# A result row for every choice of a token: plain scatters, six rows summed in the tail, three experts by one-hot products

## The reference, cut to what matters

```python
scores = sigmoid(xt @ router_w)                          # 512 x 64
_, sel = lax.top_k(scores + router_bias, 6)
wsel = scores[sel] / sum(scores[sel]) * 2.5
# each expert e, for the tokens that chose it:
gu = x[tok] @ w_gate_up[e]                               # 1024 -> 512
h = silu(gu[:, :256]) * gu[:, 256:]
y = (h @ w_down[e]) * w                                  # 256 -> 1024
routed[tok] += y
x = layer_norm(ALPHA * x + (routed + shared), ln2_g, ln2_b)
```

## Time and profile before

| | us |
|---|---|
| median of three runs | 1338.55 (1337.31 to 1342.82) |
| profiled execution, its own time | 1341.28 |
| its span on the core | 1339.6 |
| TensorE busy | 1238.4 (92%) |
| VectorE, ScalarE, GpSimd busy | 457.9, 311.3, 398.5 |
| 16 DMA engines, hardware queue of SP | 52.4% |
| 16 DMA engines, software queue of GpSimd | 7.8% |

### The profile page before, as it was taken

The page is one execution under the profiler, slowest core; times in us unless marked ns, Lnnn a source line. Parts: engine busy times, 40 slices in busy tenths (PEclk is TensorE's granted clock), DMA queues, the critical chain, the costliest instruction groups (busy, mean ns, idle before and its releaser), DMA issues.

```text
span 1339.6 us, 23794 instructions
## 1 busy us (share of the span) xinstructions
PE 1238.4 (92%) x8545; PEld 778.1 (58%) x8546; DVE 457.9 (34%) x923; ACT 311.3 (23%) x829; POOL 398.5 (30%) x424
## 2 busy tenths in 40 slices
PE   8999999999999989999999999987789979979896
PEld 5587778877774458888558654443344435534442
DVE  3755665556415443323248211111011111101115
ACT  3332333423313442222231111011111011101111
POOL 2545534355504340000000333233223322233321
PEclk9999999999999999999999899988899999989998
DMA  4621112115024223335904599999999998999995
GB/s 129 185 62 55 55 47 70 55 55 172 1 64 122 57 58 96 85 95 188 422 34 141 214 379 402 399 394 397 395 405 396 397 398 347 353 400 397 393 339 197
DMA packets 117965, 296.42 MB, mean 221 GB/s; under 512 B 11976, under 2 KB 81736, under 8 KB 101360
## 3 DMA queue, kind: packets, MB, share of 16 engines
q1 hardware_dynamic: 100384, 267.75, 52.4%
q0 software_dynamic: 15344, 25.12, 7.8%
q10 hardware_dynamic: 2144, 2.22, 0.5%
HBM read 280.93 MB, written 26.51 MB: 230 GB/s over the span
## 4 chain that ended last, share of the span: by engine, by line
PE 35%; DMA 21%; DVE 3%; issue 3%; POOL 1%; POOLq 0%; SPq 0%; ACT 0%; DVEq 0%; ACTq 0%
PE bank L1380 11%; PE bank L1980 10%; DMA sum_rows<-expert_y,row_col 8%; DMA expert_gu<-in_expert_w_gate_up_dram 6%; PE bank L1987 5%; PE bank L1386 4%; DMA sum_rows<-over_y,over_row_col 4%; DMA expert_down<-in_expert_w_down_dram 2%; PE bank L1972 1%; PE bank L2054 1%; PE bank L1408 1%; PE bank L2032 1%; PE bank L1401 1%; DMA gathered_x<-x_rows,tok_col 0%; DVE x_rows L2246 0%
## 5 line engine op out<-in xcount | busy, mean ns | idle before, releaser
L1980 PE MATMUL bank<-expert_gu,gathered_xT 128*64 128x256 f32 x2016 | 250.1, 400 | 31.7 <-DMA expert_gu<-in_expert_w_gate_up_dram 21.7
L1980 PEld LDWEIGHTS bank<-expert_gu,gathered_xT 128*64 128x64 f32 x2016 | 141.3, 138 | 121.8 <-issue 22.3
L2180 DVE SCALAR_TENSOR_TENSOR hidden<-gate,slot_w,bank 128x128 f32<-128x128 f32 x64 | 22.2, 347 | 434.1 <-ACT gate L2138 423.0
L1987 PE MATMUL bank<-expert_down,hiddenT 128*64 128x512 f32 x504 | 126.4, 623 | 18.7 <-issue 18.0
L1877 POOL DMA_INDIRECT sum_rows<-expert_y,row_col x62 | 98.2, 1584 | 47.9 <-POOL row_col L1874 46.3
L486 PE MATMUL bank<-x_high,w_head_low 128*128 128x512 f32 x224 | 93.8, 419 | 0.0
L486 PE MATMUL bank<-x_low,w_head_high 128*128 128x512 f32 x224 | 93.4, 417 | 0.0
L486 PE MATMUL bank<-x_high,w_head_high 128*128 128x512 f32 x224 | 93.4, 417 | 0.0
L1874 POOL COPY row_col<-row_idx 128x1 int32 (+1 forms) x62 | 12.0, 194 | 258.3 <-DMA sum_rows<-expert_y,row_col 136.9
L2149 ACT COPY expert_y<-bank 128x512 f32<-128x512 f32 x63 | 36.9, 585 | 180.2 <-PE bank L1987 104.3
L2138 ACT ACTIVATE gate<-bank 128x128 f32<-128x128 f32 x64 | 17.9, 279 | 247.9 <-PE bank L1980 247.9
(11 more groups left out here) (388 smaller groups left out, 2233.5 us busy)
## 6 DMA issues: line engine op xcount, KB each, us to landing
expert_gu<-in_expert_w_gate_up_dram SPq DMA_DIRECT2D x63, 2048.0 KB
expert_down<-in_expert_w_down_dram SPq DMA_DIRECT2D x63, 1024.0 KB
w_head<-in_w_in_dram SPq DMA_DIRECT2D x32, 512.0 KB, 3.9
w_tile<-in_w_in_dram SPq DMA_DIRECT2D x14, 512.0 KB, 4.2
x_rows<-in_x_dram SPq DMA_DIRECT2D x8, 512.0 KB, 6.5
sum_rows<-zero_rows SPq DMA_DIRECT2D x2, 2048.0 KB, 12.1
w_tile<-in_w_branch_a_dram SPq DMA_DIRECT2D x7, 512.0 KB, 5.7
w_pair<-in_w_in_dram SPq DMA_DIRECT2D x6, 512.0 KB, 5.5
```

What stands on the lines that cost most here:

```text
L1980: mm = nc.tensor.matmul(bank[parts[a], 0:2 * P], x[:, c, part], halves[:, a, :, :], start=(c == 0), stop=(c == KC - 1))
L1987: mm = nc.tensor.matmul(bank[parts[a], :], hidden_t[:, c * BLK:(c + 1) * BLK], dn[:, c, a * (D // 2):(a + 1) * (D // 2)], start=(c == 0), ...
```

## The change

- The two sum tensors become one, `choice_rows`, with 6 x 1024 half rows: every token has its own rows for each of its six choices. `tok` gets 512 k added for choice k, so `row_idx` points at the choice's own row; the token lists are masked back to the token with a bitwise and.
- The scatter is plain: no `compute_op`, and no wait for the scatter two steps before. The same holds for overflow blocks.
- Zeroing: six pieces of 2 MB, one in each round of the head loop.
- `DIRECT = 3`: experts 61, 62 and 63 go by one-hot products. Each result is split in a high part (ScalarE) and a rest (VectorE, `low_y`), and the products run in fp32r.
- Tail: SP loads for each tile four rows a token (`late`), then two (`first_rows`). GpSimd adds three of the six (`add_middle`), VectorE adds two to `xs` (`add_first`), and TensorE adds the remaining one and both sums into the banks (`finish_tile`). VectorE's order is add 0, add 1, normalise 0, add 2, normalise 1, add 3, normalise 2, normalise 3.

```diff
+TOKEN_BITS = int(OOB) | SEQ - 1
+TOKEN_HALF_BITS = 2 * int(OOB) | SUMS - 1
...
+            sp.wait_ge(zero_ready, 1)
             with sp.Fori(2, HEADS) as m:
...
-            sp.wait_ge(zero_ready, 1)
-            for a in sums:
-                n = a.shape[0] // P
-                sp.dma_start(a.rearrange("(n p) c -> p n c", p=P),
-                             zero[:, :].unsqueeze(1).broadcast_to([P, n, D // 2])).then_inc(zeroed, 16)
+                sp.dma_start(choice_rows[bass.ds(m * SUMS - 2 * SUMS, SUMS), :].rearrange("(n p) c -> p n c", p=P),
+                             zero[:, :].unsqueeze(1).broadcast_to([P, SUMS // P, D // 2])).then_inc(zeroed, 16)
...
-            sp.wait_ge(zeroed, 32)
+            sp.wait_ge(zeroed, 16 * TOPK)
...
-            mm = nc.vector.tensor_scalar(T["tok_idx"][part, :], ps[4][part, bass.ds(a, NE // 2, 2)], OOB, None, ALU.add)
-        mm.then_inc(idx_ready, 1)
+            then(nc.vector.tensor_scalar(T["tok_idx"][part, :], ps[4][part, bass.ds(a, NE // 2, 2)], OOB, None, ALU.add))
+        nc.vector.tensor_scalar(T["tok_idx"][:, :], T["tok_idx"][:, :], TOKEN_BITS, None, ALU.bitwise_and).then_inc(idx_ready, 1)
...
-    DIRECT = 2
+    DIRECT = 3
...
+    by_choice = choice_rows.rearrange("(k t p a) c -> t p k (a c)", k=TOPK, t=TT, p=P)
+    late = [at(f"late_rows{t}", [P, 4, D], r) for t, r in enumerate(("dnT", "bias", "dnl", "xh"))]
+    middle_rows, last_rows = [r[:, 0:3, :] for r in late], [r[:, 3:4, :] for r in late]
...
         for t in range(TT):
-            sp.dma_start(even_sums[:, t, :], token_rows[0][t, :, :]).then_inc(sums_in[0][t], 16)
-        for k in (1, 3):
-            sp.wait_ge(scattered[k], 16 * (NE // GROUP - k // 2))
-        for t in range(TT):
-            sp.dma_start(odd_sums[:, t, :], token_rows[1][t, :, :]).then_inc(sums_in[1][t], 16)
+            if t == 3:
+                sp.wait_ge(h_psum[1], NE // GROUP)
+            sp.dma_start(late[t][:, :, :], by_choice[t, :, 2:TOPK, :]).then_inc(late_in[t], 16)
+            if t == 2:
+                sp.wait_ge(y_psum[1], NE // GROUP)
+            if t == 3:
+                sp.wait_ge(h_psum[2], NE // GROUP)
+            sp.dma_start(first_rows[t][:, :, :], by_choice[t, :, 0:2, :]).then_inc(first_in[t], 16)
...
             pool.wait_ge(y_ready[k], now)
-            if not alone:
-                before, then_ = block_at(i, s - 2)
-                pool.wait_ge(scattered[before], 16 * then_)
...
-                out=sums[s % 2][:, :], out_offset=bass.IndirectOffsetOnAxis(ap=col2[:, k:k + 1], axis=0),
-                in_=y[:, k, :], in_offset=None, bounds_check=last_row, oob_is_err=False,
-                compute_op=ALU.add).then_inc(scattered[k], 16)
+                out=choice_rows[:, :], out_offset=bass.IndirectOffsetOnAxis(ap=col2[:, k:k + 1], axis=0),
+                in_=y[:, k, :], in_offset=None, bounds_check=last_row, oob_is_err=False).then_inc(scattered[k], 16)
...
+        def add_middle(t):
+            pool.wait_ge(late_in[t], 16)
+            for k in range(1, 3):
+                if k > 1:
+                    pool.wait_ge(middle_added, 2 * t + 1)
+                nc.gpsimd.tensor_tensor(middle_rows[t][:, 0, :], middle_rows[t][:, 0, :], middle_rows[t][:, k, :],
+                                        ALU.add).then_inc(middle_added, 1)
...
+        for t in range(TT - 1):
+            add_middle(t)
+        add_beta(0)
+        add_middle(TT - 1)
+        add_beta(1)
...
+        def direct(t, n, start=False):
+            pe.wait_ge(y_low, n + 1)
+            for part in (y_high[n], y_rest[n]):
+                for a in range(2):
+                    nc.tensor.matmul(z_banks[t][a][:, :], hot_row[parts[a], n, t * P:(t + 1) * P].bitcast(F32R),
+                                     part[parts[a], :].bitcast(F32R), start=(start and part is y_high[n]), stop=False)
...
+        def finish_tile(t):
+            pe.wait_ge(late_in[t], 16)
+            add_rows(t, last_rows[t][:, 0, :])
+            pe.wait_ge(middle_added, 2 * t + 2)
+            add_rows(t, middle_rows[t][:, 0, :])
+            pe.wait_ge(first_added, 2 * t + 2)
+            add_rows(t, xs[:, t, :], True).then_inc(z_psum, 1)
...
+        def low_y(s):
+            k, now = block_at(TURNS - 1, s)
+            n = s - (STEPS - DIRECT)
+            dve.wait_ge(y_ready[k], now)
+            nc.vector.tensor_tensor(y_rest[n][:, :].bitcast(F32R), ps[6 + k % 2][:, :], y_high[n][:, :],
+                                    ALU.subtract).then_inc(y_low, 1)
...
+        def add_first(t):
+            dve.wait_ge(first_in[t], 16)
+            for k in range(2):
+                if k:
+                    dve.wait_ge(first_added, 2 * t + 1)
+                nc.vector.tensor_tensor(xs[:, t, :], xs[:, t, :], first_rows[t][:, k, :], ALU.add).then_inc(first_added, 1)
```

More of the change, by code:

```diff
@@ L1898, in later @@
                     gather_later(j + 2, j + 2)
-                    if not alone:
-                        before, then_ = block_at(i, s - 3)
-                        pool.wait_ge(scattered[before], 16 * then_)
                     pool.wait_ge(over_y, j + 2)
@@ L1915, in turn @@
                     gather(i + 1, s // 2)
-                later(i, s, first and s < 3)
+                later(i, s)
                 if not (first and s == 0) and not (last and s > STEPS - DIRECT):
-                    scatter(i, s - 1, first and s < 3)
+                    scatter(i, s - 1)
         def first_gather(q):
@@ L2109, in tensor @@
+        pe.wait_ge(rows_ready, 5)
+        for n in (1, 0, 2):
             for t in range(TT - 1):
-                direct(t, n)
+                direct(t, n, n == 1)
+        finish_tile(0)
         pe.wait_ge(over_added, 1)
-        for n in range(DIRECT):
-            direct(TT - 1, n)
-        for t in range(TT - 1):
-            rows(t)
-        for t in range(TT - 1):
-            odd(t)
-        rows(TT - 1)
-        odd(TT - 1)
+        for n in (1, 0, 2):
+            direct(TT - 1, n, n == 1)
@@ L2121, in scalar @@
+        for t in range(1, TT):
+            finish_tile(t)
     def scalar(act):
@@ L2132, in later, with take_y, turn @@
                     nc.scalar.copy(yo[:, :], shared[:, :]).then_inc(over_y, 1)
-        def turn(i, first=False):
+        def take_y(b, direct):
+            out_y = y_high[b - (GROUP - DIRECT)][:, :].bitcast(F32R) if direct else y[:, b, :]
+            nc.scalar.copy(out_y, ps[6 + b % 2][:, :]).then_inc(y_ready[b], 1)
+        def turn(i, first=False, last=False):
             for s in range(STEPS):
@@ L2148, in turn @@
                         act.wait_ge(scattered[b], 16 * (then_ - 1))
-                    nc.scalar.copy(y[:, b, :], ps[6 + b % 2][:, :]).then_inc(y_ready[b], 1)
+                    take_y(b, last and s > STEPS - DIRECT)
                 act.wait_ge(h_psum[k], now)
@@ L2158, in scalar @@
         act.wait_ge(scattered[b], 16 * (then_ - 1))
[L2159 removed]
+        take_y(b, True)
         nc.scalar.preload_act_table_set(LN_EXP)
@@ L2213, in turn @@
                 later(i, s)
+                if last and s > STEPS - DIRECT:
+                    low_y(s - 1)
                 if shared_too and s < TT:
@@ L2328, in program @@
         x1_rows = nc.dram_tensor("x1_rows", [SEQ, D], F32, kind="Internal").ap()
-        sums = [nc.dram_tensor(f"sum_rows{n}", [SUMS, D // 2], F32, kind="Internal").ap() for n in range(2)]
+        choice_rows = nc.dram_tensor("choice_rows", [TOPK * SUMS, D // 2], F32, kind="Internal").ap()
         attention = ctx.enter_context(ExitStack())
```

103 lines of the change are left out of this document (52 added, 51 removed).

## The result

| | before | after |
|---|---|---|
| median, us | 1339.33 (1337.31 to 1342.82) | 1326.08 (1322.56 to 1327.03) |
| profiled execution, own time / span | 1341.28 / 1339.6 | 1322.56 / 1320.9 |
| last down weights used at (span time) | 1304.06 | 1269.73 |
| from there to the end | 35.5 | 51.2 |
| software queue, 740 to 1300 us before, 740 to 1260 us after | 17.7% of 560 us | 12.6% of 520 us |

The ratio is 0.9857 with a 95% interval of 0.9823 to 0.9891: faster by 13 us. The profiled execution is the lowest of the four timed ones, 3.5 us under their median, and the one of the kernel before lies 2.0 us over its own, so the 18.7 us between their spans are 5.5 us more than the change is worth.

The account below looks back on a forecast made before the run. Full DMA engines were taken to bound the expert stage. Stage -28.5 and routing +0.6 put the last weights at 1276.2, reads landed 1306.4, then 16.7: span 1323.1, 16.5 less, 1322 us at the median; 8 in 10: 1308 to 1339.

Parts of the forecast that it names:

- The saving in the stage: Expert stage, 741 to 1304 us: plain scatters free the DMA engines, 28.5 us less time (24 to 34).
- the lock: Tail: VectorE's adds shut out by GpSimd's; 0.5 us per clash, 1.2 us taken in all (0 to 4.7).
- The price of accumulation: Expert stage: accumulating scatters cost twice a plain write; dropping accumulation saves 33 us of engine time (29 to 37).
- The rival in which a plain scatter keeps its price: Expert stage: 2 KB pieces to scattered rows cost 5.5 us per MB even without accumulating; 1351 us, chance 0.07.
- the deduction of 3.5 for TensorE's stretches: Expert stage: in 62 us where TensorE was the limit, 3.5 of the 32 us saved buy nothing.
- more gained: Expert stage: TensorE's stretch shrinks too, as ScalarE's scatter waits go; 12 us more, 1310 us, chance 0.11.
- No gap behind the weights: Start of tail: expert 60's scatter lands at 1298 to 1304 us, as weights run out; reads follow without gap.
- The reads: Tail: 12.58 MB read back at 2.47 us per MB, 31.1 us, plus 0.5 for the last landing.
- the rival of slow reads: Tail: rows 2 MB apart read at 5.5 us per MB, 1360 us; half of that, 1341; chance 0.06.
- The rival of a compute tail: Tail: TensorE, VectorE or GpSimd falls behind the reads, or TensorE's clock drops; 12 us more, 1334, chance 0.14.
- Ahead of the stage: Before the expert stage: zeroing 12.6 MB in the head loop is free; routing's three VectorE steps cost +0.6 us.
- The one-hot products: Tail, TensorE: 48 fp32r products with half the rows take 10.7 to 21.4 us, hidden under the reads; 0 counted.

Follow-up runs that it names:

- no_sixty: The changed kernel with expert 60's scatter left out, its contribution missing from the sum; 1321.41 us, ratio 0.9844, 3.5 us less than the changed kernel beside it.

## Why the prediction was right, and where its steps were not

The forecast was 1322 us and the measurement 1326.08; the profiled span was forecast at 1323.1 and was 1320.9. The direction and the mechanism were right. The saving in the stage, the gap ahead of the reads and the lock were mis-sized, a fall of the clock was not looked at, and the errors cancel in part.

- **The price of accumulation: right.** Forecast 33 us of engine time (29 to 37); adding the flag to the changed kernel costs 35. The software queue came to 12.6% (12 was forecast). The rival in which a plain scatter keeps its price, 1351 us, falls: plain ones cost 2.58 us per MB, the lower of the two prices that the forecast took from plain writes.
- **A support of it that was none.** I read the 11.0 MB between HBM counts and packets as one more reading of the scattered rows. After the change the difference is 289.32 + 34.64 - 312.94 = 11.0 again, without accumulation. The kernel before with plain scatters shows the very counts of the earlier trace rows, and the kernel that scatters nearly nothing has 12 MB less in packets and the same HBM counts as the changed one. These counts move when a transfer is taken out of the program (0.26 MB less is written in no_sixty) and not with what the indices do at run time, so they can't tell anything of an indirect transfer. The right conclusion stood on the queue's price per MB alone.
- **The stage: -28.5, a little too little.** The last down weights are used 34.3 us earlier in the profiles, but 1.0 of that lies ahead of the token lists and 3.0 is the clock at the first products. That leaves 30.4, which is also what the kernel before with plain scatters shows (its stage starts at the low clock too); between the two kernels whose stage starts at the full clock, the changed one and the one with the flag put back, it is 32.9. Of the 35 us of engine time that were saved, 2 to 5 did not arrive, so the deduction of 3.5 for TensorE's stretches was of the right size, and the term was short because the saving was. In the stretch meant, the DMA share rose to 0.95, from 0.90 before and 0.88 with accumulation, but not to 1. The "more gained" rival (12 us more) isn't borne out, and the wait for the scatter two steps before is worth nothing, since putting that back changed nothing that the times show. The next relief would be worth half, as the experiment without scatters shows.
- **No gap behind the weights: wrong.** I put the landing of expert 60's scatter against the use of the last weights, as if they ran out when they are used. In the earlier trace rows they did: the last down product waits for its weights. After the change TensorE is the limit there (`<-issue`, no weights waited for): the last down weights have landed at 1266.76 us, 3.0 us ahead of their use. The engines run empty one by one (share 0.85 from 1262 to 1263 us, 0.49 from 1264 to 1265, 0.01 from 1266 to 1267), and the scatter, 8.0 us from issue to landing, is what SP waits for. The sum was not hurt, since the lead of the weights hid it: the rows flow from 1268.2 us, 1.5 us ahead of the last down weights' use, where I had 1.4. But 3 to 4 us that were there to be had lie in the gap. A faster stage uncovered a latency that the slower one hid.
- **The reads: right.** From the first packet to the last landing they take 32.2 us, for 31.6 forecast (31.1 and 0.5 for landing); 100.2% of 33 us for 13.1 MB is 2.52 us per MB, against 2.47 in the earlier trace rows. Rows 2 MB apart cost nothing that can be seen, so the rival of slow reads falls. The rule of the Trainium skill, DMA: Bandwidth & Descriptors, that was weighed there (by its ratio, an estimate of 8 us more) did not show in this access, in which neighbouring partitions lie 4 KB apart.
- **The lock: 1.2 us taken, 3.7 in the last two adds and 1.8 ahead of them.** I sized it from one row as 0.5 us for one meeting, and misread that row. The two instructions behind it, from the kernel before:
```profile
1327.97 2.34 POOL L1957 TENSOR_TENSOR x_rows<-x_rows,ln_b_row 128x1024 f32<-128x1024 f32 x1 [0.47 <-ACT x_rows L2169]
...
1329.58 1.95 DVE L2254 SCALAR_TENSOR_TENSOR x_rows<-x_rows,ln_mv,ln_b_row 128x512 f32<-128x512 f32 x2
```
  VectorE's step starts when the GpSimd add has 0.7 us left, so 0.5 us is the wait for the rest of an add and not the price of a meeting. After the change five of the eight adds take 3.25 to 3.35 us and one 2.91, where one alone takes 1.22: 2.0 to 2.1 for a full meeting. By the rule of the Trainium skill, SBUF — State Buffer, "Who interferes with whom", the term was up to 2.35 for each of two adds, and the trace agrees with it. Behind the last landing (1300.45 us) VectorE is still at the tile before and begins the last adds at 1302.28, 1.8 us late; they take 6.19 us for 2.5; normalise(2) takes 4.3 for 4.9. In all 20.4 us follow the last landing instead of 16.7. The upper bound of 4.7 held for the two adds (3.7), not for them and the late start together (5.5). The rival of a compute tail was right in that VectorE and GpSimd together fall behind, and wrong in its size (12 us); the granted clock is 1.00 while TensorE waits for rows (1268 to 1301 us), and falls only at 1308.9.
- **Ahead of the stage: free, as said.** The stretch of the earlier trace rows now has a DMA share of 0.33 and the same TensorE time. In routing the three steps take 0.63 us for the 0.39 of the two, so 0.2 and not 0.6 more; the lists are ready at 739.92 us, but over the profiled executions of the changed kernel and its variants that time goes from 739.4 to 743.2.
```profile
100.00:290.00 190.00, 186.19 (x2091) 145.90 (x2091) 113.15 (x236) 63.01 (x208) 92.22 (x69) 1.00 0.33 103
```
- **The one-hot products: cheaper than their bounds.** 48 of them take about 6 us (0.23 us from one pair to the next) where I had 10.7 to 21.4; they are hidden either way.

Summed over the profiled execution, against a forecast span of 1323.1: the last down weights are used 6.5 us earlier than forecast (1269.7 for 1276.2), of which 3.0 is the clock, 1.6 lies ahead of the stage and 1.9 in the saving. From there to the last landing are 30.7 us instead of 30.2, and behind it 3.7 more. That is 2.2 us less, 1320.9. At the medians, where the two profiled executions' luck does not count, the change is worth 13.3 us and not 16.5, and the forecast is 4 us low. That the point came out near is in part luck, since errors of both signs met; the direction and the range are what the working supported.

## What to carry to other kernels

Price a queue in microseconds of the engines per MB and compare kinds of transfer: here the flag `compute_op` doubled the price of a scatter (5.44 us per MB for 2.58), and one row of its own for each contribution, zeroed where the DMA engines are idle, was the cheaper way although the tail reads three times as much. When a stage gets faster, look again at the latencies that its slack covered: the first load behind it may wait for a landing that was hidden before. And where VectorE and GpSimd add from SBUF at the same time, count what is left of the GpSimd instruction when VectorE's starts, up to the whole of it, and not the mean of a few rows. Before a difference of two profiled executions is put down to a change, compare the granted clock in the same stretch of both.

## What the runs showed of the hardware that I had not expected

- GpSimd's issue of an indirect DMA depends on its kind: 1.58 us each when accumulating, 0.99 when plain; with the flag back in the changed kernel it is 1.57. Over 61 scatters that is 36 us of GpSimd's time. The plain ones:
```profile
L1885 POOL DMA_INDIRECT choice_rows<-expert_y,row_col x61: 979/991/1042, 762.4 to 1258.9; - x61
```
- Accumulating scatters of 2 KB rows moved one row a packet, 178 ns each. Plain ones moved two rows in a packet of 4096 B, 168 ns, or one row and a skipped slot in one of 2052 B, 86 ns: 2.58 us of the 16 engines per MB, as much as the plain writes of the earlier trace rows and less than those of the earlier trace rows (2.93). Skipped slots cost little: 2852 of the 8704 (68 scatters of 128) have no row, and a record with nothing but such slots has 8 B and takes 9 to 10 ns.
- One fall of the granted clock to 1.2 GHz for 6.8 us, among the stage's first products, comes with a first result that is 3.0 us later (22.7 for 19.7 us), in a stage that is otherwise bound mostly by the DMA engines.
- Fp32r products with 64 rows follow each other in pairs at 0.23 us for 512 columns each:
```profile
1272.17 0.39 PE L2113 MATMUL bank<-direct_high,hot_row 64*128 64x512 f32 x2
...
1272.40 0.40 PE L2113 MATMUL bank<-direct_low,hot_row 64*128 64x512 f32 x2
```
